# Query and key norms: the head sums of squares as two short-format products, the second part made by GpSimd, and the bias additions spread between them

## The chip, the cores and the metric

One core of one Trainium2 chip. The metric is the device time in microseconds (us) of one execution, as the median of several runs. The engines are TensorE (PE; its weight loads are listed as PEld), VectorE (DVE), ScalarE (ACT), GpSimd (POOL) and SyncE (SP, here only a queue of transfers).

## The reference

A backbone block of four layers over 256 latent tokens and 256 context tokens, 1024 channels. Layers 0 and 3 mix tokens by neighbourhood attention (16 heads of 64), layer 1 by retention, layer 2 by a convolution module; each is followed by a gated feed-forward network with a short convolution. Every sub-layer is RMS-normed and modulated by a conditioning vector. All is float32. The change is in the first part of the attention layers:

```
q, k, v = split(h @ w_qkv)
q = q * rsqrt(mean(q * q over the head's 64) + 1e-6) * q_gain     # k likewise
s_nb  = q . k_neighbours * 64 ** -0.5 + bias                      # 8 x 16 neighbourhood
s_ctx = q . k_context * 64 ** -0.5
o = softmax([s_nb, s_ctx]) @ [v_neighbours, v_context]
```

In layer 3, the last, only the latent tokens need queries; keys and values are made for both streams.

## The kernel before, in words

Activations lie with channels on the partitions and tokens along the free dimension: 8 chunks of 128 channels by 512 tokens (256 context, then 256 latent). A float32 product is made of three products in a short format (float32r, one pass through PE each): high part times high part, low times high, high times low (`three`, L672 to L674; with the activations stationary, for the V stage, L678 to L680). Each weight group of 128 x 1024 is loaded into one of four slots (`raw`, L507 by SP, when PE has used the group before it in that slot), copied to its high part `Whi` by ACT (L1186), and subtracted from it to the low part `Wlo` by DVE (L1568, "the weight split"), three groups ahead of PE. A product with both operands in plain float32 is possible too, the long format; it appears in the trace as two records.

**The query and key stage** is 16 tiles, tile k in `na` (L877 for PE, L1259 for ACT, L1793 for DVE). Tiles 0 to 7 are the keys, 8 to 15 the queries, each 128 channels, which is two heads. A wide tile covers 512 tokens; in layer 3 tiles 8 to 15 are narrow, 256 tokens. They go in four bodies of four; m is the tile's place in its body, and its accumulator is PSUM bank m. Per tile:

1. PE: 24 short-format products into bank m (`tile`).
2. ACT: the square of the bank into `na_sq[m % 2]` (L1284).
3. PE: the head sum, one long-format product of the square with `one_head` (a matrix of ones in two 64 x 64 blocks) into bank 4 or 5 (`head_sum`, L884). It is issued one tile later, behind the products of tile k + 1; the sum of the last tile of a body follows at once.
4. ACT: the root into `na_root` (`root_of`, L1266), behind the square of tile k + 1, then that tile's weight split (L1186).
5. DVE: the reciprocal (L1803), then bank m times gain times reciprocal into `QK` (L1805), which frees the bank; then the weight split for three tiles ahead (L1568).

At the start of the stage tiles are made together: in layer 0 `first_tiles` makes tiles 0, 1, 2 and half of 3 as their input chunks arrive, then comes the sum of tile 0, a conditioning slice, the rest of tile 3, and the sums of tiles 1 and 2. In layer 3 `three_tiles` makes tiles 0, 1 and 2 together, then the sums of tiles 0 and 1 follow each other, tile 3, and the sums of tiles 2 and 3. In layer 0 each body also holds a conditioning slice: 16 products with loads from `ada_ring` (`ada_slice`, L771) behind the sum of the body's first tile, and four transposes (`ada_cols`, L785) between the sum of its third tile and that of its fourth. SP issues the slice's four loads (L499) once the weight loads of the body before are issued and the slice before is used.

The V stage follows: `tokens_major` waits for the banks of tiles 12 and 13 before its first products and of 14 and 15 before its second half.

**GpSimd's part** is `pairs_staged` (L560). The relative position bias is loaded in two halves of eight heads by twelve transfers each (L575, rows of 256 bytes, issued by GpSimd itself); behind each half stand eight additions (L580), two operands of 128 x 384 in SBUF, which put `rel_in` (reversed) plus the mask into `rel`. The second half's transfers wait until the first half's additions are done, as they reuse `rel_in`. DVE waits for both halves behind tile 15 (`rel_ready`).

## Time and profile before

| | us |
|---|---|
| Runs (3) | 2506.68, 2507.7, 2511.91 |
| Median | 2507.7 |
| Profiled execution: span from first to last instruction | 2503.2 |
| Query and key stage in layer 0, first square to the last (61.86 to 158.02) | 96.2 |
| Query and key stage in layer 3, first square to the first V product (2107.00 to 2174.80) | 67.8 |

The profile gives one execution by its span; it has no separate total. The median of the runs is 4.5 us above that span. Busy shares of the whole span: PE 97%, DVE 73%, ACT 43%, GpSimd 26%. The times in the views are counted from the start of the span. A timeline row gives start, length, engine, line, operation, what it writes and reads, and how many of them; in brackets stands how long the engine was idle before it and which instruction released it. The end of a PE product is modelled, so two products overlap in the records; the distance of their starts is their cost.

### The profile page before, as it was taken

What the parts mean: (1) busy time and instruction counts of PE and PEld (TensorE: products, weight loads), DVE (VectorE), ACT (ScalarE), POOL (GpSimd) and SP (SyncE); (2) the same over time, 40 slices, a digit from 0 to 9 for tenths busy, and PEclk for the clock granted to TensorE, in tenths of its full rate; (3) what the DMA queues carried; (4) which work ended last, traced back from release to release, by engine and by line L of the source; (5) the groups of instructions that cost most, each with busy time, mean ns of one, the idle gap of its engine ahead of it and who ended that gap; (6) DMA issues with size and microseconds to landing.
All of it is one profiled execution on the core that took longest, in us unless ns stands there. A gap on an engine that the chain in (4) does not pass through costs nothing. (4 is left out here: it accounts for less than half of the span.)

```text
span 2503.2 us, 36222 instructions
## 1 busy us (share of the span) xinstructions
PE 2433.3 (97%) x12655; PEld 2003.5 (80%) x12655; DVE 1816.1 (73%) x2653; ACT 1065.2 (43%) x1679; POOL 652.6 (26%) x442
## 2 busy tenths in 40 slices
PE   7998899999999999999999999999999999998999
PEld 4675588888888868888888888778888888867999
DVE  4886569888974355427888768987988876855874
ACT  3335534443231244414444227863544324455543
POOL 2414233332300020022333224844333324101000
PEclk9999999999999999999999999999999999999999
DMA  7642025555633321224545542213555554312555
GB/s 270 178 167 76 10 84 171 173 172 192 220 103 101 103 74 51 96 98 135 174 169 173 181 142 77 67 33 111 169 175 168 185 176 125 120 51 68 186 183 186
DMA packets 94890, 337.48 MB, mean 135 GB/s; under 512 B 11840, under 2 KB 13632, under 8 KB 94656
## 3 DMA queue, kind: packets, MB, share of 16 engines
q1 hardware_dynamic: 67136, 240.38, 28.7%
q10 hardware_dynamic: 24768, 86.74, 10.5%
q0 software_dynamic: 2880, 8.92, 1.7%
q8 instruction: 70, 1.15, 0.2%
q14 instruction: 36, 0.29, 0.0%
HBM read 334.95 MB, written 1.05 MB: 134 GB/s over the span
## 5 line engine op out<-in xcount | busy, mean ns | idle before, releaser
L672 PE MATMUL bank<-Hhi,Whi 128*128 128x512 f32 (+1 forms) x2416 | 866.2, 359 | 25.2 <-DVE Wlo L1568 8.4
L674 PE MATMUL bank<-Hhi,Wlo 128*128 128x512 f32 (+1 forms) x2416 | 853.5, 353 | 0.0
L673 PE MATMUL bank<-Hlo,Whi 128*128 128x512 f32 (+1 forms) x2416 | 853.1, 353 | 0.0
L1568 DVE TENSOR_TENSOR Wlo<-raw,Whi 128x1024 fp32r<-128x1024 f32 x424 | 636.4, 1502 | 225.0 <-ACT Whi L1186 207.2
L1186 ACT ACTIVATE Whi<-raw 128x1024 fp32r<-128x1024 f32 x424 | 448.1, 1059 | 749.2 <-DMA raw<-in_weights 695.4
L672 PEld LDWEIGHTS bank<-Hhi,Whi 128*128 128x128 f32 x2416 | 457.1, 189 | 104.1 <-issue 30.5
L673 PEld LDWEIGHTS bank<-Hlo,Whi 128*128 128x128 f32 x2416 | 457.4, 189 | 63.8 <-issue 2.6
L674 PEld LDWEIGHTS bank<-Hhi,Wlo 128*128 128x128 f32 x2416 | 457.4, 189 | 63.0
L545 POOL TENSOR_TENSOR cond_w<-cond_w,cond 128x1024 f32<-128x1024 f32 x107 | 259.3, 2423 | 599.8 <-DVE square L1592 514.7
L672 PE MATMUL bank<-Ghi,Whi 128*128 128x512 f32 (+1 forms) x770 | 268.5, 349 | 0.0
L674 PE MATMUL bank<-Ghi,Wlo 128*128 128x512 f32 (+1 forms) x770 | 266.7, 346 | 0.0
L673 PE MATMUL bank<-Glo,Whi 128*128 128x512 f32 (+1 forms) x770 | 264.9, 344 | 0.0
L537 POOL TENSOR_TENSOR square<-X 128x512 f32<-128x512 f32 (+1 forms) x51 | 80.5, 1578 | 449.9 <-DVE X L1748 441.4
L674 PEld LDWEIGHTS bank<-Ghi,Wlo 128*128 128x128 f32 x770 | 144.5, 188 | 20.3
L673 PEld LDWEIGHTS bank<-Glo,Whi 128*128 128x128 f32 x770 | 144.5, 188 | 19.6
L672 PEld LDWEIGHTS bank<-Ghi,Whi 128*128 128x128 f32 x770 | 144.7, 188 | 17.5
L1592 DVE SCALAR_TENSOR_TENSOR hb<-cond_w,cond 128x1024 f32<-128x1024 f32 x113 | 155.4, 1376 | 3.8
L1506 ACT ACTIVATE hb<-hb 128x512 f32<-128x512 f32 (+1 forms) x88 | 51.0, 580 | 210.5 <-DVE hb L2111 210.5
L1592 DVE SCALAR_TENSOR_TENSOR square<-cond_w,cond 128x1024 f32<-128x1024 f32 x99 | 121.2, 1225 | 11.7
L1203 ACT ACTIVATE cond_w<-cond_w 128x1024 f32<-128x1024 f32 x107 | 112.5, 1051 | 37.6 <-POOL cond_w L545 36.3
L643 POOL TENSOR_TENSOR pooled<-pooled,products 128x512 f32<-128x512 f32 x68 | 105.1, 1545 | 33.1 <-ACT products L1469 24.5
L1803 DVE RECIPROCAL na_root<-na_root 128x512 f32<-128x512 f32 (+1 forms) x32 | 94.3, 2947 | 19.1 <-ACT na_root L1266 19.1
(267 smaller groups left out, 2990.8 us busy)
## 6 DMA issues: line engine op xcount, KB each, us to landing
raw<-in_weights SPq DMA_DIRECT2D x424, 512.0 KB, 3.4
cond_w<-in_ada ACTq DMA_DIRECT2D x160, 512.0 KB, 3.8
ada_raw<-in_ada SPq DMA_DIRECT2D x16, 512.0 KB, 16.0
ada_ring<-in_ada SPq DMA_DIRECT2D x16, 512.0 KB, 7.4
rel_in<-in_rpb POOLq DMA_DIRECT2D x48, 128.0 KB, 4.8
decay_t<-in_dist POOLq DMA_DIRECT2D x4, 640.0 KB, 4.3
X<-in_x ACTq DMA_DIRECT2D x1, 2048.0 KB, 10.7
out_y<-X SPq DMA_DIRECT2D x1, 1024.0 KB, 4.8
```

The costliest lines, as they stand in the source:

```text
L537: g.tensor_tensor(square[:, c % 2, tok], X[:, c, tok], X[:, c, tok], ALU.mult).then_inc(sum_step, 1)
L545: g.tensor_tensor(w, w, cond[:, 0, :], ALU.mult).then_inc(cond_scaled, 1)
L643: g.tensor_tensor(pooled[:, c % 2, :], pooled[:, c % 2, :], products[:, i % PRODUCTS, :], ALU.add).then_inc(pool_added, 1)
L672: t.matmul(dst, Whi[:, st.slot, w], hi, start=start, stop=False)
L673: t.matmul(dst, Whi[:, st.slot, w], lo, start=False, stop=False)
L674: return t.matmul(dst, Wlo[:, st.slot, w], hi, start=False, stop=stop)
L1186: a.activation(Whi[:, st.slot, :], raw[:, st.slot, :], ACT.Copy).then_inc(hi_split, 1)
L1203: a.activation(w, w, ACT.Copy, accum_out=cond_sum[:, n % COND_SLOTS, 0:1]).then_inc(cond_summed, 1)
L1506: a.activation(cv[:, k, tok], cv[:, k, tok], ACT.Gelu_apprx_tanh).then_inc(gelu_done, 1)
L1568: v.tensor_tensor(Wlo[:, st.slot, :], raw[:, st.slot, :], Whi[:, st.slot, :].bitcast(F32), ALU.subtract)\
L1592: last = v.scalar_tensor_tensor(scratch, w, 1.0, cond[:, r, :], ALU.mult, ALU.mult, accum_out=cond_sum[:, slot, r:r + 1])
L1803: v.reciprocal(na_root[:, m, tok], na_root[:, m, tok]).then_inc(qk_rstd, 1)
```

## The change

For tiles with m below 3, other than tiles 1 and 2 of layer 0, ACT squares the bank a second time, behind the root of the tile before, into `sq_hi` in the short format, which keeps the high part. GpSimd subtracts it from the full square, in place of the square (`sq_lo` lies where `na_sq` does), and PE makes the head sum of two short-format products, high and low, with a short-format copy of `one_head` that ACT makes once per attention layer. That is 10 tiles in layer 0 and 12 in layer 3, six of them narrow. The other 10 sums stay as they were. There is one `sq_hi`. On GpSimd's queue the subtraction of tile k stands ahead of the additions of step q = k modulo 8; the eight additions of a half, which were one batch, are made two at a time in steps 2 to 5, the wait for the bias transfers stands in step 2, and the transfers of the second half stand behind step 7 of the first. The diff:

```diff
--- before.py
+++ after.py
@@ -275,6 +275,10 @@
         _, rel_in = region(("na_qk", [P, 2 * C * T], F32), ("rel_in", [P, NA_HEADS // 2 * 6, GRID_W], F32))
         _, na_sq, na_root = region(("na_skip", [P, 2 * C * T + TB * D + CTX + NA_HEADS * 6 * GRID_W], F32),
                                    ("na_sq", [P, 2, T], F32), ("na_root", [P, 4, T], F32))
+        _, sq_lo = region(("sq_skip", [P, 2 * C * T + TB * D + CTX + NA_HEADS * 6 * GRID_W], F32),
+                          ("sq_lo", [P, 2, T], F32R))
+        _, sq_hi, one_head_r = region(("hi_skip", [P, 2 * C * T + NA_HEADS // 2 * 6 * GRID_W], F32),
+                                      ("sq_hi", [P, T], F32R), ("one_head_r", [P, P], F32R))
         QKr, Vr, On, decay_t = region(
             ("QKr", [P, 2 * C, T], F32), ("Vr", [P, TB, 2 * D], F32), ("On", [P, TB, 2 * D], F32),
             ("decay_t", [P, 2, DIST_W], F32))
@@ -342,6 +346,9 @@
         h_hi = sem("h_hi")
         h_ready = sem("h_ready")
         qk_squared = sem("qk_squared")
+        head_copied = sem("head_copied")
+        sq_high = sem("sq_high")
+        sq_low = sem("sq_low")
         qk_summed = sem("qk_summed")
         qk_root = sem("qk_root")
         qk_rstd = sem("qk_rstd")
@@ -425,6 +432,18 @@
         def sum_first(r):
             return sum(sum_steps(q) for q in range(r))
 
+        FP32_FIRST = (1, 2)
+
+        def in_parts(layer, m, k):
+
+            return m < 3 and not (layer == 0 and k in FP32_FIRST)
+
+        def parts_before(layer, nth, m, i):
+
+            if layer == 0:
+                return sum(in_parts(0, q % 4, q) for q in range(8 * nth + 4 * i + m))
+            return 12 - len(FP32_FIRST) + 6 * nth + m + 3 * i
+
         def ctx_first(r):
             return sum(HALVED[:r])
 
@@ -556,6 +575,16 @@
                     add_square(r, whole, whole, CT)
                     pool.wait_ge(tile_free, FREE0 + tile0 + 1 + whole)
                     add_square(r, whole + 1, whole, XT)
+
+            def square_low(layer, k):
+
+                nth, i, m = k // 8, k // 4 % 2, k % 4
+                if in_parts(layer, m, k):
+                    tok = XT if layer == DEPTH - 1 and nth else ALL
+                    pool.wait_ge(qk_squared, 2 * C * (layer // 3) + k + 1)
+                    pool.wait_ge(sq_high, parts_before(layer, nth, m, i) + 1)
+                    g.tensor_tensor(sq_lo[:, m % 2, tok], na_sq[:, m % 2, tok], sq_hi[:, tok].bitcast(F32),
+                                    ALU.subtract).then_inc(sq_low, 1)
 
             def pairs_staged(layer):
 
@@ -573,12 +602,16 @@
                             src = bass.AP(rpb.tensor, at, [[1, GRID_W], [RPB_H * RPB_W, some], [1, GRID_W]])
                             dst = rel_in[:, :, :].rearrange("p (h a) k -> p h a k", a=6)
                             g.dma_start(dst[64 * par:64 * par + 64, :, a, :], src).then_inc(rel_loaded, 16)
-                    pool.wait_ge(rel_loaded, 16 * 12 * (2 * j + half + 1))
-                    if half == 0:
-                        pool.wait_ge(const_loaded, CONSTS_IN)
                     for q in range(some):
-                        last = g.tensor_tensor(rel[:, some * half + q, :, :], rel_in[:, 6 * q:6 * q + 6, ::-1],
-                                               mask[:, None, :].to_broadcast([P, 6, GRID_W]), ALU.add)
+                        square_low(layer, 8 * half + q)
+                        if q == 2:
+                            pool.wait_ge(rel_loaded, 16 * 12 * (2 * j + half + 1))
+                            if half == 0:
+                                pool.wait_ge(const_loaded, CONSTS_IN)
+                        for pair in ((2 * q - 4, 2 * q - 3) if 2 <= q < 6 else ()):
+                            last = g.tensor_tensor(rel[:, some * half + pair, :, :],
+                                                   rel_in[:, 6 * pair:6 * pair + 6, ::-1],
+                                                   mask[:, None, :].to_broadcast([P, 6, GRID_W]), ALU.add)
                     last.then_inc(rel_ready, 1)
 
                 pool.wait_ge(rel_ready, 2 * j + 2)
@@ -879,10 +912,18 @@
                 last_layer = layer == DEPTH - 1
                 qk0 = 2 * C * j
 
-                def head_sum(k_static, k, tok):
-                    pe.wait_ge(qk_squared, qk0 + k + 1)
-                    t.matmul(bank[4 + k_static % 2][:, tok], one_head[:, :], na_sq[:, k_static % 2, tok],
-                             start=True, stop=True).then_inc(qk_summed, 1)
+                def head_sum(m, nth, i, tok):
+                    k = 8 * nth + 4 * i + m
+                    dst = bank[4 + m % 2][:, tok]
+                    if in_parts(layer, m, k):
+                        pe.wait_ge(head_copied, j + 1)
+                        pe.wait_ge(sq_low, parts_before(layer, nth, m, i) + 1)
+                        t.matmul(dst, one_head_r[:, :], sq_hi[:, tok], start=True, stop=False)
+                        last = t.matmul(dst, one_head_r[:, :], sq_lo[:, m % 2, tok], start=False, stop=True)
+                    else:
+                        pe.wait_ge(qk_squared, qk0 + k + 1)
+                        last = t.matmul(dst, one_head[:, :], na_sq[:, m % 2, tok], start=True, stop=True)
+                    last.then_inc(qk_summed, 1)
 
                 for nth, tok in ((0, ALL), (1, XT if last_layer else ALL)):
                     for i, first in ((0, True), (1, False)) if layer == 0 else peeled(pe, 2):
@@ -891,11 +932,11 @@
                         together = first and nth == 0
                         if together and layer == 0:
                             first_tiles(p, steps)
-                            head_sum(0, 0, tok)
+                            head_sum(0, 0, 0, tok)
                             ada_slice(0)
                             first_tile(steps[3], 3, range(4, C))
-                            head_sum(1, 1, tok)
-                            head_sum(2, 2, tok)
+                            head_sum(1, 0, 0, tok)
+                            head_sum(2, 0, 0, tok)
                             ada_cols(ADA_START)
                         elif together:
                             three_tiles(p["mix_tile"], steps[:3], p["mix_ready"], 2 * layer)
@@ -904,12 +945,12 @@
                             if not (together and m < 3):
                                 tile(p["mix_tile"] + k, m, [(steps[m], C)], Hhi, Hlo, tok)
                             if m:
-                                head_sum(m - 1, k - 1, tok)
+                                head_sum(m - 1, nth, i, tok)
                             if layer == 0 and n < ADA_QK and m == 1:
                                 ada_slice(n)
                             if layer == 0 and n < ADA_QK and m == 3:
                                 ada_cols(ADA_START + n)
-                        head_sum(3, 8 * nth + 3 + 4 * i, tok)
+                        head_sum(3, nth, i, tok)
                 if layer == 0:
                     pe.wait_ge(mod_ready, 4 * ADA_FIRST)
                 tokens_major(p["v"], 2, p["mix_tile"] + 16)
@@ -1274,6 +1315,10 @@
 
                 if layer:
                     a.preload_act_table(ACT.Sqrt)
+                else:
+                    act.wait_ge(const_loaded, CONSTS_IN)
+                    act.wait_ge(ada_rows_made, 4)
+                a.activation(one_head_r[:, :], one_head[:, :], ACT.Copy).then_inc(head_copied, 1)
                 for nth, tok in ((0, ALL), (1, XT if last_layer else ALL)):
                     for i in bodies(act, 2, layer == 0):
                         for m in range(4):
@@ -1284,6 +1329,8 @@
                             a.activation(na_sq[:, m % 2, tok], bank[m][:, tok], ACT.Square).then_inc(qk_squared, 1)
                             if m:
                                 root_of(m - 1, k - 1, tok)
+                            if in_parts(layer, m, k):
+                                a.activation(sq_hi[:, tok], bank[m][:, tok], ACT.Square).then_inc(sq_high, 1)
                             if layer or st.n:
                                 split(st)
                         root_of(3, 8 * nth + 3 + 4 * i, tok)
```

## Rows read from the trace of the kernel before

**Rows 1.** The page, part 1: busy us (share of the span) and instructions.
```profile
span 2503.2 us, 36222 instructions
...
PE 2433.3 (97%) x12655; PEld 2003.5 (80%) x12655; DVE 1816.1 (73%) x2653; ACT 1065.2 (43%) x1679; POOL 652.6 (26%) x442
```

**Rows 2.** Timeline of ACT, layer 3: squares of tiles 4, 5 and 6.
```profile
2124.72 0.60 ACT L1284 ACTIVATE na_sq<-bank 128x512 f32<-128x512 f32 x1 [4.21 <-PE bank L674]
...
2130.16 0.60 ACT L1284 ACTIVATE na_sq<-bank 128x512 f32<-128x512 f32 x1 [3.90 <-PE bank L674]
...
2136.51 0.60 ACT L1284 ACTIVATE na_sq<-bank 128x512 f32<-128x512 f32 x1 [3.86 <-PE bank L674]
```

**Rows 3.** Timeline of PE, layer 0: second and fourth conditioning slice, next tile's first product.
```profile
86.80 1.91 PE L771 MATMUL bank<-ada_ring,csilu 128*32 128x512 f32 x12
...
90.17 0.50 PE L672 MATMUL bank<-Hhi,Whi 128*128 128x512 f32 x1
...
144.01 1.92 PE L771 MATMUL bank<-ada_ring,csilu 128*32 128x512 f32 x16
145.86 0.50 PE L672 MATMUL bank<-Hhi,Whi 128*128 128x512 f32 x1
```

**Rows 4.** Stretches (busy PE, PEld, DVE, ACT, POOL; clock, DMA share, GB/s); GpSimd's queue, 71 to 92.
```profile
71.00:91.00 20.00, 18.82 (x80) 11.71 (x79) 19.79 (x14) 7.05 (x10) 8.55 (x13) 1.00 1.00 235
...
105.00:110.00 5.00, 5.00 (x24) 4.11 (x23) 4.96 (x4) 0.43 (x2) 0.00 (x0) 1.00 1.01 401
...
q0 software_dynamic: 560, 1.55, 36.6%
```

**Rows 5.** Timeline of DVE, layer 3: reciprocals of tiles 0, 1, 6; eviction of tile 13.
```profile
2111.82 3.35 DVE L1803 RECIPROCAL na_root<-na_root 128x512 f32<-128x512 f32 x1 [1.61 <-ACT na_root L1266]
...
2117.13 3.35 DVE L1803 RECIPROCAL na_root<-na_root 128x512 f32<-128x512 f32 x1
...
2144.45 3.35 DVE L1803 RECIPROCAL na_root<-na_root 128x512 f32<-128x512 f32 x1 [0.21 <-ACT na_root L1266]
...
2174.22 0.48 DVE L1805 SCALAR_TENSOR_TENSOR QK<-bank,qk_gain,na_root 128x256 f32 x1 [0.17 <-DVE na_root L1803]
```

**Rows 6.** Timeline of PE, layer 3: sums of tiles 0 and 1; first V product.
```profile
2110.04 1.88 PE L884 MATMUL bank<-na_sq,one_head 128*128 128x512 f32 x4
...
2174.80 0.47 PE L678 MATMUL bank<-Whi,Hhi 128*128 128x512 f32 x1 [1.44 <-DVE QK L1805]
```

**Rows 7.** Timeline of ACT, layer 3: square and root of tile 0.
```profile
2107.00 0.60 ACT L1284 ACTIVATE na_sq<-bank 128x512 f32<-128x512 f32 x1 [1.26 <-PE bank L674]
...
2111.10 0.69 ACT L1266 ACTIVATE na_root<-bank,eps 128x512 f32<-128x512 f32 x1 [2.06 <-PE bank L884]
```

**Rows 8.** One line's instructions: GpSimd additions of layer 2, ns min/median/max.
```profile
L643 POOL TENSOR_TENSOR pooled<-pooled,products x68: 1273/1303/2102, 1534.9 to 1651.1; 128x512 f32<-128x512 f32 x68
```

**Rows 9.** Two holes of PE, the stretches behind them, and the stretch around V's start.
```profile
904.14 7.12 PE L1005 MATMUL bank<-QKr 128*128 128x512 f32 x16 [2.25 <-DVE hb L1943]
...
904.00:908.00 4.00, 3.86 (x5) 1.56 (x6) 2.64 (x6) 1.89 (x3) 2.63 (x4) 0.59 0.07 14
...
1565.91 0.47 PE L672 MATMUL bank<-Hhi,Whi 128*128 128x512 f32 x1 [2.70 <-DVE Wlo L1568]
...
1568.00:1572.00 4.00, 4.00 (x14) 3.12 (x14) 4.00 (x5) 3.44 (x10) 3.71 (x3) 0.71 0.00 0
...
2172.00:2176.00 4.00, 2.52 (x11) 1.56 (x10) 3.83 (x5) 3.70 (x6) 0.00 (x0) 1.00 0.42 131
```

**Rows 10.** Weight splits of layer 3: two beside GpSimd; nine of 2140 to 2175.
```profile
2108.58 1.62 DVE L1568 TENSOR_TENSOR Wlo<-raw,Whi 128x1024 fp32r<-128x1024 f32 x1 [3.41 <-ACT Whi L1186]
...
2137.23 1.71 DVE L1568 TENSOR_TENSOR Wlo<-raw,Whi 128x1024 fp32r<-128x1024 f32 x1
...
L1568 DVE TENSOR_TENSOR Wlo<-raw,Whi x9: 1212/1216/1226, 2143.0 to 2174.6; 128x1024 fp32r<-128x1024 f32 x9
```

**Rows 11.** Timeline of GpSimd, layer 0: second batch of bias loads.
```profile
71.74 8.11 POOL L575 DMA_DIRECT2D rel_in<-in_rpb  x12 [0.29 <-POOL rel L580]
```

## The prediction

> **What bounds the kernel now.** I read the page first: TensorE (PE) is busy 97% of a span of 2503.2 us [rows 1], so in most stages a microsecond taken from PE is one taken from the end, and the question is only where this stage is an exception. The change touches the query and key tiles of layers 0 and 3, so next I read the times at which ScalarE (ACT) begins its square, once per tile. Two wide tiles (512 tokens) with no head sum between them are 5.44 us apart, and two with one sum between them 6.35 us [rows 2]; layer 0's tiles have the same shape. So a head sum in the long format holds PE for 0.91 us and each of a tile's 24 short-format products for 5.44 / 24 = 0.227 us. In layer 0 PE is the bound, with one hole: the second conditioning slice. From its first product to the next tile it takes 3.37 us, where the clean slice of a later body takes 1.85 us [rows 3]; it waited 1.52 us for its load. In that stretch the DMA engines are full, and GpSimd's own queue, which carries only the position bias, takes 36.6% of 20 us, or 7.3 us of all engines [rows 4].
>
> Layer 3 is the exception. There VectorE (DVE) works without a break from the reciprocal of tile 0 at 2111.82 to the query/key eviction of tile 13 at 2174.22. The one wait is 0.21 us before tile 6's reciprocal at 2144.45 [rows 5], and PE's first V product waits for that eviction, at 2174.80 [rows 6]. A wide tile costs DVE 5.3 us (2111.82 to 2117.13), a narrow one 3.45 us: from 2144.45 to 2174.22 less two wide periods and 1.9 us of reciprocal, over five. PE in layer 3 gains nothing by finishing early; it loses only if it feeds DVE late.
>
> **The sums themselves.** 22 of 32 sums become two products in the short format: 2 x 0.227 = 0.45 us for 0.91, or 0.45 us saved at 512 tokens. Layer 0 has ten of them, all on PE's path. One in each of the last three bodies stands before a long-format sum that waits for the new square, but four transposes lie between the two, so nearly nothing is lost: 4.4 us. The bounds: nothing saved if two more waits leave PE a bubble at each sum, 4.5 us if none.
>
> **The second square, ACT.** 22 squares more, 0.60 us each when wide, by the row of the first one [rows 7]. ACT is busy 43% [rows 1] and waits for PE between tiles, so they cost nothing by themselves. They come after the previous tile's root, before the weight split, and push the split by 0.5 us; DVE then still has a reciprocal ahead of it. The copy of the head matrix (128 columns) is one short activation, in layer 0 ahead of the first tile, in layer 3 behind the table load, both times while ACT waits for PE: nothing.
>
> **The subtraction, GpSimd.** 22 of them, 1.30 us when wide by the nearest row of the same form [rows 8], about half when narrow. From the end of a tile: square 0.8, root about 0.6, second square 0.6, subtraction 1.3, with hand-overs 3.6 us. The sum comes a whole tile (5.44 us) later, so it is hidden wherever a tile lies between, in layer 3's narrow tiles by DVE's period of 3.45 us. If GpSimd were late by more than the 1.8 us left, PE would stand.
>
> **Where no tile lies between: layer 3, tile 1.** In layer 0 tiles 1 and 2 keep the long format; in layer 3 they don't, and the sums of tiles 0 and 1 follow each other directly. ACT squares tile 0 at 2107.00 [rows 7]; its low part is ready at about 2109.6, before PE begins the sum at 2110.04 [rows 6]: no wait. Its root began at 2111.10 [rows 7], now 0.45 us earlier, 2110.65. Behind the root (0.6) comes the second square of tile 1 (0.6), then the subtraction (1.3): 2113.3. PE stands from 2110.5, with tile 3 queued behind the waiting sum, and starts that tile at 2113.75. Before, it started it at 2110.04 + 2 x 0.91 = 2111.86. Late by 1.9 us.
>
> A hole of 2.8 us has a second price. The only two holes of over 2 us behind the first hundred, 2.25 and 2.70 us long, are each followed by a granted clock under full speed: 0.59 over 904 to 908 (four microseconds at 0.59 are 1.64 us lost) and 0.71 over 1568 to 1572; around the 1.44 us hole before the V stage [rows 6] it stays at 1.00 [rows 9]. I take 1.7 us, PE at its lower level for some 3.4 us; the other bound is none.
>
> Both reach tile 6's reciprocal, where DVE already waits for PE: 1.9 + 1.7, less two sums of 0.45 on PE's path (tiles 4 and 5), less 0.3 for tile 6's own (its root waits behind tile 7's square, so not all of 0.45 counts), less nothing for tile 2 (the long sum behind it waits for a square that ends 0.87 us after). That is +2.3 us; without the fall of the clock +0.6.
>
> **The additions, spread.** Same number, same length. What moves is whom they meet. A weight split takes DVE 1.22 us, but 1.62 and 1.71 us beside GpSimd's additions in layer 3; from 2140 on GpSimd has no work, and all nine splits lie between 1.212 and 1.226 us [rows 10]. After the change six subtractions and eight additions, some 12 us of GpSimd work, fall into the 27 us of layer 3's narrow tiles, and DVE is the bound there. Of the seven splits between tile 6 and tile 13 about four meet one and lose 0.4 us each, the mean of the two rows (0.45): +1.5 us. The bounds are none and 7 x 1.0 = 7 us, an addition's length for each; I stay by the rows, since DVE waits only for the rest of an addition already begun. The Trainium skill (SBUF — State Buffer, Who interferes with whom) speaks against this change: a VectorE instruction with two SBUF inputs and a GpSimd one that reads SBUF shut each other out for the whole instruction, and the order of issue decides. By that rule alone a split issued just behind each operation would make the term 7 us; the rows show the same exclusion at 0.4 us a meeting. In layer 0 and in the wide tiles of layer 3 DVE has room for it.
>
> **The moved DMAs.** The second batch of twelve bias loads leaves at 71.74 and takes 8.11 us to issue [rows 11]. Now it stands behind the last addition and the subtractions of tiles 4 to 6, so it leaves near 97 us, and in layer 3 near 2142 instead of 2116. The slice load that came late is then free of it: 7.3 us of engine time less, the 1.52 us wait goes. The next slice load meets the batch instead, but it leaves about 2.5 us later than the batch. The rest of the batch (5 us), that load (2.1 MB, 5.2 us at the 401 GB/s which such loads reach alone [rows 4]) and one weight load (1.3 us) are through at about 111 us, an estimate, and PE wants the first quarter at 112.4. I take nothing, up to 3 us if the order is bad. DVE waits for the bias only after tile 15; the last additions are done some 10 us earlier.
>
> **Sum.** Layer 0: -4.4 - 1.5 = -5.9. Layer 3: +2.3 + 1.5 = +3.8. Together -2.1 us on the profiled span, whose 2503.2 us lie 4.5 us under the median of 2507.7; I apply it to the median: 2505.6 us. What a measurement of this kernel can tell from no change is about 0.2%, 5 us.
>
> **Rivals.**
> - *The clock holds.* The hole is PE's only idle time there and the fall may miss it. Then layer 3 costs +2.1 and the total is -3.8: 2503.9 us. Against it, both holes over 2 us fell; for it, they are only two.
> - *Layer 3 costs nothing.* If GpSimd subtracts sooner than its row says, or DVE's backlog swallows the hole and the splits miss the additions, at most +0.3 is left: -5.6, 2502.1 us, faster. Against: DVE has no slack at tile 6 [rows 5].
> - *The moved batch hits the loads that matter; slower.* In layer 3 it leaves as the narrow tiles begin, where a weight group is used every 3.45 us, not 5.44. DVE is two tiles, 6.9 us, behind PE (tile 13 evicted when all 16 are done), so a load may be late by about that. ACT, though, waits for loads in order, with the squares behind. From a delay of about 7 us on it decides, and then the batch's 7.3 us come through: +7.3 in layer 3, and a slice wait of 4.5 us in layer 0 (1.5 and the 3 of above). -5.9 + 4.5 + 3.8 + 7.3 = +9.7: 2517.4 us. Against: in layer 3 there is no slice load beside it.
> - *The short pair saves nothing*, because of bubbles at its waits: -1.5 + 3.8 + 0.95 (tiles 4, 5 unsaved) = +3.2: 2510.9 us.
>
> **How the numbers follow.** Forecast 0.43, clock holds 0.24 (0.03 of it beyond 5 us), layer 3 free 0.17, moved batch 0.11, no saving 0.05 (0.01 beyond). Faster by over 0.2%: 0.20; slower: 0.12; within: 0.68. The range runs from just under the third case, 2501.5, to 2510.5, and leaves out the batch's case and the tails.
>
> **What would show it.** Squares 5.9 us apart instead of 6.35 across a converted sum in layer 0; no wait for the second slice's load; PE idle about 2.8 us near 2104 (2110 less the 6 gained) behind GpSimd's subtraction, then a clock near 0.6 for four microseconds; the time from tile 0's reciprocal to the V stage in layer 3 3 to 4.5 us longer, several narrow splits over 1.3 us. The forecast is wrong if layer 3's stage is no longer than before, if ACT waits for weight loads in it, or if layer 0's stage shortens by less than 4 us.

## The result and the profile after

The changed kernel takes 2511.43 us (median of 20 runs, 2509.63 to 2513.73), the kernel before in the same session 2506.93 (20 runs, 2503.73 to 2511.91). The ratio is 1.0018 [1.0013, 1.0024]: 4.5 us slower, where the forecast was 2 us faster. The profiled execution has a span of 2508.1 us against 2503.2. The page, part 1, as [rows 1]:

```profile
span 2508.1 us, 36313 instructions
PE 2432.7 (97%) x12655; PEld 2008.0 (80%) x12655; DVE 1820.5 (73%) x2653; ACT 1073.3 (43%) x1703; POOL 680.7 (27%) x464
```

PE is busy for as long as before (2432.7 us for 2433.3) in a span 4.9 us longer: it stands more. Only the places tell more.

**The squares, layer 0.** ACT's timeline of the changed kernel, tiles 8 to 11 (start us, us, engine line operation, in brackets the idle time before it and what ended it):

```profile
106.32 0.60 ACT L1329 ACTIVATE na_sq<-bank 128x512 f32<-128x512 f32 x1 [4.60 <-PE bank L707]
...
111.76 0.60 ACT L1329 ACTIVATE na_sq<-bank 128x512 f32<-128x512 f32 x1 [3.41 <-PE bank L707]
...
124.19 0.60 ACT L1329 ACTIVATE na_sq<-bank 128x512 f32<-128x512 f32 x1 [4.44 <-PE bank L707]
...
130.13 0.60 ACT L1329 ACTIVATE na_sq<-bank 128x512 f32<-128x512 f32 x1 [3.34 <-PE bank L707]
```

Across a converted sum two squares are 5.94 us apart (124.19 to 130.13), where the kernel before had 6.35 [rows 2]: a short pair saves 0.40 us. But from tile 9 to tile 10, around the third conditioning slice, it is 12.43 us, against 8.41 in the kernel before (115.41 to 123.82) and 7.98 around the second slice (85.09 to 93.07), whose load now came in time. What stood in that gap, on PE, GpSimd and in the stretches (columns as in [rows 4]):

```profile
112.11 1.81 PE L804 MATMUL bank<-ada_ring,csilu 128*32 128x512 f32 x8
116.20 1.05 PE L804 MATMUL bank<-ada_ring,csilu 128*32 128x512 f32 x4 [2.28 <-DMA ada_ring<-in_ada]
117.43 1.05 PE L804 MATMUL bank<-ada_ring,csilu 128*32 128x512 f32 x4 [0.18 <-DMA ada_ring<-in_ada]
...
94.88 1.29 POOL L586 TENSOR_TENSOR sq_lo<-na_sq,sq_hi 128x512 fp32r<-128x512 f32 x1 [3.77 <-ACT sq_hi L1333]
96.11 8.10 POOL L604 DMA_DIRECT2D rel_in<-in_rpb  x12
...
99.55 2.10 SPq L518 DMA_DIRECT2D ada_ring<-in_ada  x4
```

```profile
100.00:105.00 5.00, 5.00 (x22) 3.77 (x21) 4.86 (x6) 1.72 (x3) 4.21 (x7) 1.00 1.02 258
105.00:110.00 5.00, 5.00 (x24) 4.14 (x23) 4.96 (x4) 2.03 (x3) 1.29 (x1) 1.00 1.05 221
110.00:115.00 5.00, 3.93 (x18) 1.77 (x16) 3.00 (x2) 1.66 (x3) 1.26 (x1) 1.00 1.03 238
```

The slice's load leaves 3.4 us behind the moved batch, as foreseen, but with both under way the DMA engines are full (share 1.02 to 1.05) and move only 221 to 258 GB/s. The last quarter comes at 117.4 and not at 111. The queues from the slice load's start to that moment (packets, MB, share of the engines' time; q0 is GpSimd's, q1 has the slice and the weights):

```profile
q1 hardware_dynamic: 920, 3.38, 66.1%
q0 software_dynamic: 457, 1.22, 36.2%
```

Of these 17.9 us the batch took 6.5 (forecast 5), and q1 11.8 for 3.38 MB (forecast 6.5 for 2.6 MB). At 401 GB/s its 3.38 MB would be 8.4 us. So, as an estimate, 1.5 us of the delay is more of the batch, 1.9 us more weight data (groups loaded at 99.01, 106.31 and 111.75, where the forecast had one), and 3.4 us the lower rate beside the batch. The stage, from tile 0's square to tile 15's eviction, is 1.08 us shorter than before (105.32 for 106.40), instead of 5.9.

**Layer 3, tile 1.** PE, ACT, GpSimd and DVE at the first sums:

```profile
2108.28 0.39 PE L921 MATMUL bank<-sq_hi,one_head_r 128*128 128x512 f32 x1
...
2111.67 0.47 PE L921 MATMUL bank<-sq_hi,one_head_r 128*128 128x512 f32 x1 [2.77 <-POOL sq_lo L586]
...
2109.53 0.59 ACT L1333 ACTIVATE sq_hi<-bank 128x512 fp32r<-128x512 f32 x1
...
2110.26 1.27 POOL L586 TENSOR_TENSOR sq_lo<-na_sq,sq_hi 128x512 fp32r<-128x512 f32 x1 [2.49 <-ACT sq_hi L1333]
...
2113.73 1.28 POOL L586 TENSOR_TENSOR sq_lo<-na_sq,sq_hi 128x512 fp32r<-128x512 f32 x1 [2.21 <-ACT sq_hi L1333]
...
2113.84 2.25 DVE L1615 TENSOR_TENSOR Wlo<-raw,Whi 128x1024 fp32r<-128x1024 f32 x1
2116.02 3.34 DVE L1850 RECIPROCAL na_root<-na_root 128x512 f32<-128x512 f32 x1
...
2133.40 3.35 DVE L1850 RECIPROCAL na_root<-na_root 128x512 f32<-128x512 f32 x1 [1.10 <-ACT na_root L1307]
...
2145.29 3.35 DVE L1850 RECIPROCAL na_root<-na_root 128x512 f32<-128x512 f32 x1 [0.56 <-ACT na_root L1307]
```

PE stands 2.77 us behind GpSimd's subtraction. One thing was not foreseen: tile 3's weight split begins 0.11 us behind tile 2's subtraction and takes 2.25 us, where a free one takes 1.22. Tile 1's reciprocal follows the split without a gap, 6.36 us behind tile 0's for 5.31 before [rows 5]. But this delay does not reach the end: DVE then stands 1.10 us before tile 4's reciprocal (2133.40) and 0.56 us before tile 6's (2145.29), each time for a root that could only be made once PE had got there. The stage is lost through PE, as forecast. The clock, behind that hole and at the V stage (third number from the end):

```profile
2112.00:2116.00 4.00, 4.00 (x12) 3.17 (x11) 3.84 (x3) 2.12 (x3) 2.27 (x2) 0.57 0.00 0
2176.00:2180.00 4.00, 3.67 (x10) 2.96 (x11) 3.83 (x5) 2.18 (x2) 0.00 (x0) 0.64 0.14 53
2180.00:2184.00 4.00, 4.00 (x18) 3.26 (x17) 3.83 (x5) 0.00 (x0) 0.00 (x0) 0.93 0.00 0
```

```profile
2176.33 0.47 PE L711 MATMUL bank<-Whi,Hhi 128*128 128x512 f32 x1 [1.59 <-DVE QK L1852]
```

Between the first hole and the second the clock was at 1.00; the second fall follows PE's wait of 1.59 us for tile 13's eviction. A third one (0.78 over 2308 to 2312) follows a wait of 1.65 us at the final norm; it cost nothing that shows: the early batch of run 4 has no fall there and takes as long from the V stage's end to the last eviction (1.8 us more than before, the changed kernel 1.9). The kernel before waits 1.44 us at the V stage and keeps its clock [rows 6, 9]. In the changed kernel the wait is longer because the split that DVE makes last before tile 13's reciprocal meets GpSimd's last additions:

```profile
2172.53 1.39 DVE L1615 TENSOR_TENSOR Wlo<-raw,Whi 128x1024 fp32r<-128x1024 f32 x1
```

It takes 1.22 us before, and in all profiles the wait follows it: 1.43 or 1.44 with a split of 1.22, 1.59 to 1.61 with 1.38 or 1.39, 1.78 with 1.57. From the first square of layer 3 to the first V product it is 71.09 us, for 67.80: +3.29. From there to the next stage's first scaling the fall adds 1.58.

**Where the time went.** DVE's last eviction comes at 2502.44, for 2497.41: +5.0 us. Start-up 0.5 us shorter; layer 0 -1.1; the layers between -0.1; layer 3's query and key tiles +3.3; V stage +1.6; from there to the end +1.9. This last is not the change: in that stretch all the profiles below, variants of the kernel before among them, take 1.2 to 3.8 us more than the one profile of the kernel before did. A single profile is a draw too, and sums of it are good to about 2 us.

### The profile page after: what moved, and what is told of

It reads as the page before. It is cut to its first block and busy times, and to the rows that moved or that the text cites. A ratio compares the mean times of both kernels' runs of the same rounds, so it can differ in the third digit from the quotient of the medians.

```text
span 2508.1 us, 36313 instructions
## 1 busy us (share of the span) xinstructions
PE 2432.7 (97%) x12655; PEld 2008.0 (80%) x12655; DVE 1820.5 (73%) x2653; ACT 1073.3 (43%) x1703; POOL 680.7 (27%) x464
## 3 DMA queue, kind: packets, MB, share of 16 engines
HBM read 334.95 MB, written 1.05 MB: 134 GB/s over the span
```

## The experiments

All compare with the kernel before, in the same session, 11 runs each (20 in the first row). Times are the kernel's and that of before, with the ratio and its interval. "Layer 0" is tile 0's square to tile 15's eviction (106.40 before), "layer 3" its first square to the first V product (67.80 before), "V" from there to the stage's end (92.74 before), all from one profile each and given as the difference to before.

| kernel | us | before | ratio | layer 0 | layer 3 | V |
|---|---|---|---|---|---|---|
| changed (first) | 2511.43 | 2506.93 | 1.0018 [1.0013, 1.0024] | -1.08 | +3.29 | +1.58 |
| changed, again | 2511.57 | 2507.68 | 1.0013 [1.0004, 1.0022] | -0.17 | +3.27 | +1.59 |
| layer 3 long | 2507.24 | 2507.51 | 0.9998 [0.9989, 1.0007] | -0.87 | 0.0 | 0.0 |
| layer 0 long | 2509.71 | 2507.51 | 1.0007 [0.9998, 1.0016] | -1.51 | +3.21 | 0.0 |
| moves alone | 2507.42 | 2507.51 | 1.0000 [0.9991, 1.0009] | -0.31 | +0.48 | 0.0 |
| early batch | 2505.13 | 2507.51 | 0.9992 [0.9983, 1.0001] | -5.53 | +1.96 | 0.0 |
| early batch, layer 3 long | 2502.41 | 2507.68 | 0.9980 [0.9971, 0.9989] | -5.56 | 0.0 | 0.0 |
| early batch, tile 1 long | 2503.84 | 2507.68 | 0.9984 [0.9975, 0.9993] | -5.57 | +3.00 | 0.0 |
| changed, hole filled | 2510.57 | 2507.68 | 1.0013 [1.0004, 1.0022] | -0.59 | +1.67 | +1.65 |
| before, batch delayed | 2508.59 | 2507.55 | 1.0005 [0.9996, 1.0014] | +0.57 | 0.0 | 0.0 |
| late batch, layer 3 long | 2508.01 | 2507.55 | 1.0003 [0.9994, 1.0012] | +0.41 | 0.0 | 0.0 |
| tile 1 long, additions last | 2502.43 | 2507.55 | 0.9985 [0.9976, 0.9994] | -5.55 | +0.99 | +1.61 |
| before, batch behind load | 2505.76 | 2507.55 | 0.9992 [0.9983, 1.0001] | -1.46 | 0.0 | 0.0 |

The three columns of a row add up to the difference of its medians within 1.3 us, but for the last but one (-3.0 by stages, -5.1 by medians): the changed kernel has +3.8 and +4.7 by stages, +4.5 and +3.9 by medians.

**1. Layer 3 long.** Its sums in the long format; layer 0 as changed.

```
-            return m < 3 and not (layer == 0 and k in FP32_FIRST)
+            return layer == 0 and m < 3 and k not in FP32_FIRST
```

> Layer 0 as in the changed kernel, layer 3 with all head sums in the long format, so its bias additions and its second batch of bias DMAs fall back to their old places. My theory (A): in layer 3 the loss comes from the short format's long way round, above all the hole of 2.8 us at tile 1 and the clock that falls behind it. Then tile 0's reciprocal to tile 13's eviction is 62.4 us again (changed kernel: 66.1), the first V product comes about 1.6 us earlier than in the kernel before, and the time is 1.6 us under it: ratio 0.9994, unless a hole that the kernel before passes at full clock is hit by a fall of the clock (1.7 us each). Rival (B): layer 3's loss comes later than the query and key tiles (the V stage and the final norm lost 1.7 and 1.9 us in the changed kernel behind holes that the kernel before has too) and belongs to the shift in time, not to the sums: then the first V product is 1.6 us early, but the end is 2 us or more late, ratio 1.0008. Rival (C): the head matrix's copy or another leftover costs: the stage of layer 3 is over 1 us longer than before.

Layer 3's stage takes 67.79 us again: its whole loss hangs on the short format there, and the copy of the head matrix costs nothing. The time is the kernel before's and not 1.6 us under it: layer 0 brings 0.87 us only, its third slice again late (12.64 us between its squares, PE waits 2.87).

**2. Layer 0 long.** The reverse.

```
+            return layer > 0 and m < 3
```

> Layer 0 with all head sums in the long format (its bias work back in its old places), layer 3 as in the changed kernel. (A): layer 0's stage ends where it did in the kernel before (0 +- 0.2 us), and the stage of layer 3 alone costs 3.3 us to its first V product: +3.3 to +5 us with the fall of the clock behind the V stage's hole: ratio 1.0013 to 1.0020. Rival: layer 3 costs only what it does because layer 0 shifted it by 1.6 us against the clock's rhythm; then the fall at tile 1 is absent or of another size, and the stage of layer 3 costs 1.5 us or less: ratio 1.0006.

Layer 3 alone costs 3.21 us, with the same hole (2.77) and the same fall of the clock: not an effect of layer 0's shift. The V stage's fall is absent. Layer 0 was expected level and came 1.51 us shorter: the second slice did not wait. There the second batch of bias loads left at 73.41, 2.25 us behind the slice's load (71.16), because GpSimd's eight additions took 8.71 us in this execution, for 7.74 before. That became the question of runs 9 and 12.

**3. Moves alone.** Long sums everywhere; GpSimd waits for the same squares, so that additions and DMAs lie where the change puts them.

```
-                    pool.wait_ge(sq_high, parts_before(layer, nth, m, i) + 1)
-                    g.tensor_tensor(sq_lo[...], na_sq[...], sq_hi[...].bitcast(F32), ALU.subtract)...
```

(shortened; besides, `in_parts` returns False, and a copy of its old condition tells GpSimd when to wait)

> All head sums in the long format, no second square's subtraction, but GpSimd waits at the same squares as in the changed kernel, so that the additions and the second batch of bias DMAs come where they do there. (A): in layer 0 the third slice's load lands at the same time as in the changed kernel, since the moved batch sets it and not PE: the second slice's wait of 1.5 us is gone, the third slice waits about 2 us in its place, and the tenth tile's square comes within 0.5 us of 124.2; the stage ends level with the kernel before. In layer 3 the meetings with weight splits cost under 1 us. Sum 0 to +1 us: ratio 1.0002. Rival (B): the moved work by itself costs the 5 us of the changed kernel (splits on DVE, loads that come late in layer 3's narrow tiles): ratio 1.0018. Rival (C): the moved work is a gain (1.5 us less wait at the second slice, nothing at the third, because PE reaches it later): ratio 0.9994.

(A), with a smaller wait: it moves from the second slice (gone) to the third (1.17 us more between its squares, 2 expected), and the sum is nothing. In layer 3 the moves cost 0.48 us. So the moved work alone is not the loss; in layer 0 it takes the gain away only once the short sums bring PE to the slice earlier.

**4. Early batch.** The first eight additions in one piece, then the second batch, in layer 0; all else as changed.

```
+                if layer == 0:
+                    bias_loads(0); squares 0-2; add_pairs(0, range(0, 8))
+                    bias_loads(1); squares 3-10; then as the change has it
```

(shortened, partly in words)

> The changed kernel, except that in layer 0 GpSimd makes the first eight additions in one piece behind tile 0's subtraction and then issues the second batch of bias DMAs, near 72 us as in the kernel before. (A): the third slice no longer waits (4 us in the changed kernel); the second slice waits for its load as in the kernel before and longer, about 2.8 us, because that load's landing is fixed while PE comes 1.3 us earlier. Layer 0's stage ends 1 to 1.5 us earlier than in the changed kernel; the time is 1.2 us under the changed kernel's: ratio to the kernel before 1.0013. Rival (B): loads bound layer 0's stage wherever the batch is put, and it ends where it does in the changed kernel (within 0.3 us): ratio 1.0018. Rival (C): the second slice's wait stays at 1.5 us: the stage ends 2.8 us earlier, ratio 1.0007.

None of the three: each had a slice wait left. Neither slice waits, and the stage is 5.53 us shorter. GpSimd and SP:

```profile
73.66 8.14 POOL L604 DMA_DIRECT2D rel_in<-in_rpb  x12 [0.29 <-POOL rel L611]
...
71.40 1.81 SPq L518 DMA_DIRECT2D ada_ring<-in_ada  x4
```

The batch leaves 2.3 us behind the second slice's load instead of beside it. In layer 3 the same hole of 2.77 us was not followed by a fall of the clock, and the stage cost 1.96 us instead of 3.3:

```profile
2108.37 0.47 PE L973 MATMUL bank<-sq_hi,one_head_r 128*128 128x512 f32 x1 [2.77 <-POOL sq_lo L586]
```

```profile
2108.00:2112.00 4.00, 3.63 (x16) 3.04 (x17) 3.84 (x3) 2.37 (x4) 1.79 (x3) 1.00 0.02 7
2112.00:2116.00 4.00, 3.78 (x17) 2.62 (x15) 4.00 (x2) 1.43 (x3) 4.00 (x4) 1.00 0.12 19
```

**5. The changed kernel again.** No edit.

> The changed kernel once more, beside the same runs of the kernel before as the next three. If the clock's falls behind PE's short holes follow from what the kernel does, this profile shows the same three in layer 3 (behind tile 1's hole, behind the V stage's, at the final norm) and a span within 0.5 us of 2508.1. If they are drawn anew in each execution, their number differs, with 1.5 to 1.9 us of span for each. Ratio in either case 1.0018 +- 0.0006.

Between the two: the falls in layer 3 are again there, all three, but a fourth came in layer 0, behind the third slice's wait, which had none in the first profile. The span is 2509.8.

```profile
116.00:120.00 4.00, 3.03 (x9) 0.49 (x9) 1.78 (x2) 0.72 (x1) 0.00 (x0) 0.60 0.74 291
```

With it that slice costs 13.36 us between squares, and layer 0's stage gains 0.17. Layer 3 costs the same 3.27 us, though here tile 3's split was first by 0.05 us, took 1.22 us (GpSimd's subtraction took 2.31 instead) and tile 1's reciprocal came 5.31 us behind tile 0's, as before. DVE waited 1.11 us before tile 4's reciprocal all the same. So the split's meeting at tile 3 is not what the stage loses.

**6. Early batch, layer 3 long.** Runs 1 and 4 together.

> The early batch of the last experiment in layer 0, and layer 3 with long-format sums throughout. (A): layer 3 costs nothing; the last experiment's layer 0 gave 5.1 us by the start of layer 3 and its layer 3 took 2.0 us back up to the V stage. So the first V product comes 5.1 us earlier than in the kernel before and the time is 2 us under the last experiment's: ratio to the kernel before 0.9984 if that one's 0.9992 holds. Rival (B): the last experiment was fast by luck with the clock (no fall at all behind 1668 us), and the combination only equals it: ratio 0.9992 or more.

2502.41 us, 5.3 us under the kernel before (ratio 0.9980) and 9.2 under the changed one beside it. (A): layer 3 costs nothing, and the interval [0.9971, 0.9989] holds its 0.9984. Its gain is clear of the noise, and no kernel here is faster (run 11 is level with it). It has ten of the 22 short sums, and the batch of bias loads behind the slice load.

**7. Early batch, tile 1 long.** Layer 3 short but for tile 1, which gets no second square and no subtraction.

```
-                if in_parts(layer, m, k):
+                if in_parts(layer, m, k) and (layer, k) != (3, 1):
```

(shortened: the counts that are waited for shift with it, and PE and ACT leave out tile 1 too)

> As the early batch, with layer 3 short except its tile 1, whose sum is one long product and waits only for its square (no second square, no subtraction for it). (A): PE's hole at tile 1 is gone, tile 1's reciprocal comes 6.4 - 5.3 = 1.1 us earlier against tile 0's than in the early-batch kernel; what is left of layer 3's cost is the narrow tiles' meetings on DVE and the earlier waits, 0.9 us. Time 1 us over the combination with layer 3 long: ratio 0.9988. Rival (B): the hole only moves: tile 2's sum waits for its own subtraction, and PE stands there for over 1 us. Rival (C): the meetings are the larger part, and the V stage comes over 1.5 us later against the start of layer 3 than in the kernel before.

The hole is gone, and tile 1's reciprocal comes 5.88 us behind tile 0's: 0.48 of the 1.05 us back, since tile 3's split (1.77 us) still meets GpSimd. And rival (C) came in: from tile 6's reciprocal to tile 13's eviction DVE lost 2.35 us, where the changed kernel loses 0.6 to 0.9 with the same instructions in the same order there. DVE's narrow splits and GpSimd's additions, in this kernel:

```profile
2153.42 1.87 DVE L1669 TENSOR_TENSOR Wlo<-raw,Whi 128x1024 fp32r<-128x1024 f32 x1
2165.36 2.02 DVE L1669 TENSOR_TENSOR Wlo<-raw,Whi 128x1024 fp32r<-128x1024 f32 x1
...
2153.20 4.89 POOL L611 TENSOR_TENSOR rel<-rel_in,mask 128x384 f32<-128x384 f32 x4
2164.33 1.97 POOL L611 TENSOR_TENSOR rel<-rel_in,mask 128x384 f32<-128x384 f32 x2
```

and in the changed kernel:

```profile
2165.34 1.36 DVE L1615 TENSOR_TENSOR Wlo<-raw,Whi 128x1024 fp32r<-128x1024 f32 x1
...
2165.58 2.95 POOL L612 TENSOR_TENSOR rel<-rel_in,mask 128x384 f32<-128x384 f32 x2
```

Here the split was first and lost 0.14 us while GpSimd's pair of additions took 2.95; there GpSimd was first, its pair took 1.97, and the split lost 0.80. Who starts first pays least. The Trainium skill (SBUF — State Buffer, Who interferes with whom) says that the order of issue decides who blocks; the two traces agree.

**8. Hole filled.** The changed kernel with ten products without use where PE stands; they start once tile 1 is squared.

```
+                                for _ in range(10):
+                                    t.matmul(bank[5][:, :], one_head_r[:, :], Hhi[:, 0, :], start=True, stop=True)
```

(shortened: the condition and the wait for the square stand above)

> The changed kernel with ten further short-format products (2.3 us) written into tile 1's own sum bank ahead of its sum, where PE stands idle for 2.8 us in layer 3; their result is overwritten by the sum. (A): the fall of the clock behind this place is caused by the idle time: with the products there the clock stays at 1.00 over 2108 to 2120, and tile 4's reciprocal keeps tile 1's distance to the kernel before (-1.1 us) instead of +0.3. The time is 1.5 us under the changed kernel's. Rival (B): the fall belongs to the point in time or to something else than PE's idleness (DMA idle, GpSimd busy): it stays, and the time is the changed kernel's. The hole itself stays 1 us long on DVE's path in both.

```profile
2111.07 2.50 PE L950 MATMUL bank<-Hhi,one_head_r 128*128 128x512 f32 x10
2114.02 0.47 PE L921 MATMUL bank<-sq_hi,one_head_r 128*128 128x512 f32 x1 [0.46 <-POOL sq_lo L586]
...
2112.00:2116.00 4.00, 3.54 (x16) 2.60 (x15) 3.84 (x2) 3.12 (x6) 1.29 (x1) 1.00 0.33 123
2116.00:2120.00 4.00, 4.00 (x19) 3.31 (x18) 4.00 (x3) 0.88 (x1) 3.92 (x3) 1.00 0.01 4
...
2116.17 2.28 DVE L1619 TENSOR_TENSOR Wlo<-raw,Whi 128x1024 fp32r<-128x1024 f32 x1
```

With PE busy the clock stays at 1.00, and layer 3 costs 1.67 us instead of 3.3. Together with run 4 (hole there, clock held, 1.96) this puts the fall at 1.3 to 1.6 us at the V stage. What remains is PE's lateness: the products do not bring the sum forward, which starts 6.46 us behind tile 0's square for 6.43. Tile 3 is squared 12.68 us behind tile 0 (10.43 before), so 2.2 us late; two short sums give 0.8 back, and tile 6's root comes 1.05 us late. DVE waits for it (0.55 us). Tile 3's split took 2.28 us again and changes nothing of that. The time fell by 1.0 us (2510.57 for 2511.57), which these runs can't tell from nothing.

**9. Before, batch delayed**, and **12. Before, batch behind load.** One wait in the kernel before, layer 0 only; for tile 2's square in run 9, for tile 3's in run 12.

```
+                        if layer == 0:
+                            pool.wait_ge(qk_squared, 3)     # run 12: 4
                     for par in range(2):
```

> The kernel before, except that in layer 0 the second batch of bias DMAs waits for tile 2's square, so that it leaves near 74 us instead of 71.7, behind the second slice's load (71.5 to 73.4 us) and not beside it. (A): the wait of 1.5 us at the second slice came from the order in the queues, not from the amount: it is gone, and all that follows comes 1.5 us earlier, ratio 0.9994. Rival (B): the early-batch kernel lost that wait because of something else (its weight loads lie differently); here the wait stays within 0.3 us: ratio 1.0000. Rival (C): the delayed batch hits the next slice (used near 107 us): a wait there in place of the one removed.

> The kernel before, as in the delayed-batch experiment, but the second batch of bias DMAs waits for tile 3's square, which comes about 1.9 us behind the start of the slice load; the last edit left it beside the load (73.41 against 73.50 us) and so tested nothing. Now the batch starts behind the load's last DMA. (A): the wait at the second slice (1.5 and 2.9 us in the two profiles with batch and load side by side) is gone or under 0.3 us, tiles 5 and 6 are squared 8.4 us apart as around a slice without a wait; layer 0's stage ends 1.5 to 2 us earlier against its first square. Ratio 0.9994. Rival (B): the wait stays over 1 us: then the early-batch kernels lost it for another reason, such as PE's earlier weight loads. Rival (C): the bias additions now end so late that they meet another transfer, and the third slice waits.

Run 9 decided nothing: tile 2's square was over before GpSimd's additions were, so the batch left at 73.41, still beside the load (73.50), and the second slice took 10.46 us between squares. In run 12 it left behind the load:

```profile
74.75 8.10 POOL L577 DMA_DIRECT2D rel_in<-in_rpb  x12 [3.18 <-ACT na_sq L1286]
...
71.77 1.84 SPq L499 DMA_DIRECT2D ada_ring<-in_ada  x4
...
86.34 0.60 ACT L1286 ACTIVATE na_sq<-bank 128x512 f32<-128x512 f32 x1 [3.90 <-PE bank L676]
94.75 0.60 ACT L1286 ACTIVATE na_sq<-bank 128x512 f32<-128x512 f32 x1 [1.80 <-PE bank L676]
```

Tiles 5 and 6 are 8.41 us apart, the time of a slice without a wait, and the stage is 1.46 us shorter: (A). One wait on GpSimd, which has time, is worth that in the profile; the medians (1.8 us) can't tell it from nothing.

**10. Late batch, layer 3 long.** Layer 0's second batch behind tile 10's subtraction; the first additions are spread as in the changed kernel.

> As the combination of early batch and long layer 3, but layer 0's second batch of bias DMAs leaves behind tile 10's subtraction, near 122 us, and its eight additions follow the last subtraction. (A): a batch costs where it leaves a few microseconds ahead of a slice load: the fourth slice's load leaves near 127 us, 5 us behind the batch, and the fourth slice waits 2 to 4 us for it (squares of tiles 13 and 14 over 10 us apart, 8.0 in the combination). Time 3 us over the combination: ratio 0.9992. Rival (B): only the third slice is sensitive, because there a weight group had also to be fetched; then nothing waits and the time equals the combination's: ratio 0.9980.

The fourth slice took the blow, 13.30 us between its squares for 7.98 without a wait, a fall of the clock (0.59) included:

```profile
143.05 3.01 PE L856 MATMUL bank<-ada_ring,csilu 128*32 128x512 f32 x8 [2.47 <-DMA ada_ring<-in_ada]
...
123.42 8.16 POOL L604 DMA_DIRECT2D rel_in<-in_rpb  x12
...
126.85 2.20 SPq L518 DMA_DIRECT2D ada_ring<-in_ada  x4
```

So it is no property of the third slice: (A), with a higher price than the 2 to 4 us expected. All cases in one table, batch start less slice load's start, and what the slice's squares are further apart than without a wait:

| kernel | batch - load, us | slice | cost, us |
|---|---|---|---|
| changed; again; filled; layer 3 long | -3.4 (four times) | third | 4.5; 5.4; 5.0; 4.7 |
| late batch | -3.4 | fourth | 5.3 |
| moves alone (slower PE) | -6.0 | third | 1.2 |
| before, batch delayed | -0.1 | second | 2.1 |
| before | +0.2 | second | 1.5 |
| layer 0 long; early batch (four profiles); behind load | +2.3; +2.3, +2.8, +2.3, +2.9; +3.0 | second | 0 |

**11. Tile 1 long, additions last.** Run 7 with layer 3's second eight additions behind the last subtraction.

> As the kernel with tile 1 long in layer 3, but layer 3's second eight additions all follow the last subtraction instead of standing between the narrow tiles'. (A): the 2.4 us that DVE lost there between tiles 8 and 12 (splits of 1.6 to 2.0 us) come from the additions: with them gone from there the splits are 1.2 us again, but for meetings with the 0.7 us subtractions, and the V stage comes 1.5 to 2.4 us earlier than in that kernel. Ratio to the kernel before 0.9976 to 0.9980. Rival (B): it is the subtractions, which stay: splits stay over 1.5 us, the time is that kernel's, 0.9984. Rival (C): the additions now run into the V stage and hold DVE's splits there: the gain is given back before attention begins.

Tiles 8 to 11 are split in 1.21 to 1.22 us, so it was the additions and not the subtractions. The three splits behind them met the additions instead (1.57, 1.62, 1.64 us), and the first V product waited 1.78 us, followed by a clock of 0.59: of the 2.0 us gained up to the V stage 1.6 went again. (A) for the cause, (C) for the place.

## Why the prediction was wrong, step by step

- **"The next slice load meets the batch instead ... I take nothing, up to 3 us."** This is the step that failed. The order was foreseen (2.5 us apart, 3.4 in the trace), but I let the three transfers go one after the other at the rate of an undisturbed load (401 GB/s), through at 111; side by side with the batch's small pieces the engines are as full and move 221 to 258 GB/s, and the last quarter came at 117.4. My own [rows 4] had this rate beside a batch, 235 GB/s at a share of 1.00. The rate is about half of the delay; the other half is that I took too little of the batch (5 us for 6.5) and one weight load where 1.3 MB were moved. The cost was 4.5 to 5.4 us, the highest with a fall of the clock behind the wait. The slower rival had put 4.5 us of slice waits into layer 0, as the second slice's 1.5 and 3 more; the size came true, all of it at the third slice.
- **Short sums, -4.4.** Right in kind, 0.40 each and not 0.45: ten bring 4.0, and with the second slice's 1.5 they are the 5.5 us of the early batch. **The second slice's wait, -1.5:** gone, as said; but it took no move of the batch by 25 us, only by 2 (run 12).
- **Layer 3, tile 1, +2.3 at tile 6.** The hole was 2.77 us for 2.8. From the stage's start to tile 6's reciprocal the kernel lost 2.6 us with the fall of the clock (the changed kernel and layer 0 long) and 1.0 without (early batch), for 2.3 and 0.6. The fall is worth 1.6 us for 1.7. The path is the one forecast: DVE waits for tile 6's root, which PE's lateness sets. PE was late by 2.2 us for 1.9, and the two sums gave back 0.8 for 0.9. The meetings of splits with subtractions in the wide tiles (2.25 us for 1.22) had the room that the forecast gave them as long as PE was late; only where the hole was taken away (run 7) did they set tile 6, and cost 0.6 us.
- **Four meetings of narrow splits, +1.5.** 0.6 to 0.9 us in the changed order, 2.4 in run 7: the term lay inside, but is decided by which of two instructions starts first by tenths of a microsecond.
- **"Around the 1.44 us hole before the V stage it stays at 1.00."** In the changed kernel that hole is 1.59 to 1.61 us and the clock fell behind it in both of its profiles and in that of the filled one (in run 2 and run 4, with 1.59 and 1.60, it did not): 1.6 us that the sum did not have. The longer wait is a split beside the last additions, 1.39 us for 1.22.
- **Moved batch in layer 3, +7.3 in the slower rival.** Not there: ACT waited 4.50 us for a weight load at 2157.19, DVE, two tiles behind, did not. The wait itself was one of the signs by which the forecast was to be wrong; it came true without costing anything. So did the other, layer 0's stage shorter by less than 4 us, and that one was the cause.
- **Second square and subtraction hidden otherwise:** held but for one: the sum at 2160.24 in layer 3 waits 1.01 us for GpSimd, behind ACT's late weight load, where PE is not the bound. No sum of layer 0 waits for it.

With 4.5 to 5.4 for nothing at the third slice and 1.6 at the V stage, the sum of -2.1 becomes +4.0 to +4.9. The median says +4.5; the smaller misses (short sums, tile 6, narrow splits) nearly cancel. What stays open: why the clock falls behind one wait and not behind the same one elsewhere, and why the end of the one profile of the kernel before was some 2 us faster than all others.

## What to carry to other kernels

When a step issues DMAs, work out at what time they leave against each load that an engine will wait for: a batch that leaves 2 to 3 us behind such a load cost nothing here, beside it 1.5 to 2 us, and 3.4 us ahead of it 4.5 us or more, whichever slice it was. Apply a cheaper form only where its engine is the bound: the short sums were worth 4 us in the stage bound by TensorE and cost 3.3 in the one bound by VectorE: 2.6 because their first wait had no cover (1.6 of it the clock), the rest because GpSimd's work met DVE's. And when holes of an engine change, count on the clock too.

## What was not expected of the hardware

- **The clock and short holes.** The granted clock fell (to its lower level of 1.2 GHz for part of the stretch) behind holes of PE of 1.59 to 1.61 us at the V stage in three profiles of five, behind the one of 1.78, and in none of the eight with 1.43 or 1.44; behind the waits of 1.50 to 2.18 us at the final norm in twelve of fourteen; behind tile 1's 2.77 us in three of four; and behind the slice waits of layer 0 with 2.41, 2.47 and 2.65 us, but not behind those with 2.28 and 2.87. Where PE was the bound or fed it, a fall cost 1.3 to 1.6 us. A hole is not needed either: in the kernel before the clock was 0.67 over 1668 to 1672 with no wait of PE over 0.8 us ahead of it, but with 24 products of two columns each (from 1665.19 to 1667.89). The same hole can go either way: the Trainium skill (TensorE: Matmul & The Clock Gate, Part 1: The HAM clock gate) says that the window in which activity is watched runs freely, so that a kernel meets it at another phase each time. These traces agree with that as far as they go: one and the same hole of 2.77 us fell in three profiles and held in the fourth.
- **Start-up.** Tile 0's square came between 59.6 and 63.8 us in the fourteen profiles, of kernels that are nearly the same up to it: 4 us of spread before anything measured here begins.
- **Full DMA engines at half the rate.** 1.02 to 1.05 of their time at 221 to 258 GB/s beside the bias loads; weight and slice loads alone reach 401 [rows 4].
